# Cached-key expansion beside prefill attention: a third squares buffer, an earlier split of the next stream, and scores issued behind the value products

## The reference

```python
def mla_expand(c_kv, w_kv_b, k_norm):
    b, S, _ = c_kv.shape
    kvb = (c_kv @ w_kv_b).reshape(b, S, MLA_HEADS, QK_NOPE + V_HEAD)   # 16 heads, 64 + 64
    k_nope = rmsnorm(kvb[..., :QK_NOPE], k_norm)
    return k_nope, kvb[..., QK_NOPE:]

def attend(q_nope, q_rope, k_nope, k_rope, v, q_pos, k_pos):
    s = (einsum(q_nope, k_nope) + einsum(q_rope, k_rope)) * ATTN_SCALE
    mask = (k_pos // CHUNK)[None, :] <= (q_pos // CHUNK)[:, None]
    p = softmax(where(mask, s, -inf), axis=-1)
    return einsum(p, v)
```

## Time and profile before

| | us |
|---|---|
| median of 3 runs (1838.54 to 1841.67) | 1838.8 |
| the profiled execution | 1838.99 |
| its span | 1837.2 |
| TensorE busy in the span | 1809.3 |
| VectorE busy | 1135.8 |
| ScalarE busy | 827.9 |
| GpSimd busy | 228.9 |

### The profile page before, as it was taken

The page is one execution under the profiler, slowest core; times in us unless marked ns, Lnnn a source line. Parts: engine busy times, 40 slices in busy tenths (PEclk is TensorE's granted clock), DMA queues, the critical chain, the costliest instruction groups (busy, mean ns, idle before and its releaser), DMA issues.

```text
span 1837.2 us, 28276 instructions
## 1 busy us (share of the span) xinstructions
PE 1809.3 (98%) x10567; PEld 1732.5 (94%) x10567; DVE 1135.8 (62%) x1706; ACT 827.9 (45%) x1420; POOL 228.9 (12%) x280
## 2 busy tenths in 40 slices
PE   9999999999999999999999999999998999999998
PEld 9999999799888999999999999996777999999998
DVE  6454447879889645444775454456778856454445
ACT  6333336665564433333553333346665544333333
POOL 1000110311311000011400001122112131000110
PEclk9999999999999999999999999999999999999999
DMA  6434444456352544454344434451124534444442
GB/s 212 135 117 136 139 138 153 153 207 235 122 206 87 193 125 127 124 149 138 115 143 118 135 116 140 139 170 40 47 85 142 166 116 127 133 120 131 143 137 76
DMA packets 68452, 249.48 MB, mean 136 GB/s; under 512 B 8264, under 2 KB 10568, under 8 KB 67088
## 3 DMA queue, kind: packets, MB, share of 16 engines
q1 hardware_dynamic: 58880, 206.86, 36.8%
q0 software_dynamic: 9488, 41.48, 6.6%
HBM read 235.51 MB, written 12.12 MB: 135 GB/s over the span
## 4 chain that ended last, share of the span: by engine, by line
PE 82%; DVE 10%; ACT 3%; DMA 2%; issue 2%; POOL 0%; SPq 0%; DVEq 0%; ACTq 0%; POOLq 0%
PE pair L1913 24%; PE pair L1914 24%; PE pair L1915 24%; DVE wlo L1245 2%; PE pair L2333 2%; PE pair L2335 2%; PE pair L2334 2%; DVE cy L1372 1%; DMA lowA<-in_cacheT 1%; DVE S L1468 1%; PE pair L2422 1%; PE pair L1920 0%; PE pair L1922 0%; PE pair L1921 0%; PE pair L2121 0%
## 5 line engine op out<-in xcount | busy, mean ns | idle before, releaser
L1913 PE MATMUL pair<-xh,whi 128*128 128x384 f32 x1960 | 660.3, 337 | 3.0 <-DVE xl L1255 2.0
L1915 PE MATMUL pair<-xh,wlo 128*128 128x384 f32 x1960 | 654.9, 334 | 0.0
L1914 PE MATMUL pair<-xl,whi 128*128 128x384 f32 x1960 | 654.8, 334 | 0.0
L1245 DVE TENSOR_TENSOR wlo<-raw,whi 128x1024 fp32r<-128x1024 f32 (+3 forms) x371 | 463.8, 1252 | 160.7 <-ACT whi L708 159.8
L708 ACT ACTIVATE whi<-raw 128x1024 fp32r<-128x1024 f32 (+2 forms) x369 | 378.0, 1028 | 261.9 <-PE pair L1915 257.8
L1913 PEld LDWEIGHTS pair<-xh,whi 128*128 128x128 f32 x1960 | 367.9, 188 | 10.0 <-DVE wlo L1245 3.9
L1914 PEld LDWEIGHTS pair<-xl,whi 128*128 128x128 f32 x1960 | 368.0, 188 | 1.6 <-issue 1.0
L1915 PEld LDWEIGHTS pair<-xh,wlo 128*128 128x128 f32 x1960 | 367.9, 188 | 0.0
L1265 DVE TENSOR_TENSOR tg<-pair,rstd 128x384 f32<-128x384 f32 x88 | 49.1, 558 | 326.2 <-PE pair L1915 325.5
L1913 PE MATMUL pair<-ah,whi 128*128 128x384 f32 x704 | 235.2, 334 | 0.0
L1914 PE MATMUL pair<-al,whi 128*128 128x384 f32 x704 | 235.1, 334 | 0.0
(11 more groups left out here) (408 smaller groups left out, 2202.2 us busy)
## 6 DMA issues: line engine op xcount, KB each, us to landing
raw<-in_stream SPq DMA_DIRECT2D x372, 512.0 KB, 3.6
S<-in_ssm POOLq DMA_DIRECT2D x4, 2048.0 KB, 9.3
out_ssm_s<-S POOLq DMA_DIRECT2D x4, 2048.0 KB, 7.8
seg<-acs_rows POOLq DMA_DIRECT2D x12, 512.0 KB, 6.0
cTb<-in_cacheT POOLq DMA_DIRECT2D x10, 512.0 KB, 4.3
kn<-rs_rows SPq DMA_DIRECT2D x16, 264.0 KB
lowC<-in_cache SPq DMA_DIRECT2D x8, 512.0 KB, 3.2
lowA<-in_cacheT POOLq DMA_DIRECT2D x6, 512.0 KB, 5.0
```

The source lines that it names most:

```text
L1245: V.tensor_tensor(wlo[:, r, 0:w], raw[:, r, 0:w], whi[:, r, 0:w].bitcast(F32), ALU.subtract).then_inc(lo_ready, 1)
L1913: M(out, whi[:, r, ws], mh_(k), start=first and k == k0, stop=False)
L1914: M(out, whi[:, r, ws], ml_(k), start=False, stop=False)
L1915: ins = M(out, wlo[:, r, ws], mh_(k), start=False, stop=last and k == k1 - 1)
```

## The change

Three edits. The squares get three slots of 512 columns in `kn` in place of two, so a square waits for the row sum of three products back. `past_split(y + 1)` moves ahead: on ScalarE from behind the output copy to the place before the square of product 8y + 3, on VectorE from behind the output's low part to the place behind the row sum of product 8y + 4. And TensorE issues the scores of two heads right behind the value products of a turn, where they stood at the head of the next turn; only heads 2 and 3 stay at the head of turn 0. Scores of turn y are thus those of heads 2y + 4 and 2y + 5.

```diff
--- before.py
+++ after.py
@@ -1077,11 +1077,11 @@
 
             def past_square(w):
                 act.wait_ge(past_ps, w + 1)
-                if w < 2:
+                if w < 3:
                     act.wait_ge(key_turn_ps, 4)
                 else:
-                    act.wait_ge(past_sum, w - 1)
-                A(kn[:, w % 2, 0:512], bank[w % 2][:, :], ACT.Square).then_inc(past_sq, 1)
+                    act.wait_ge(past_sum, w - 2)
+                A(knf[:, 512 * (w % 3):512 * (w % 3) + 512], bank[w % 2][:, :], ACT.Square).then_inc(past_sq, 1)
 
             def p_exp(x):
                 s, o = x % 2, 48 + 8 * (x % 2)
@@ -1121,6 +1121,8 @@
                 p_turned(2 * y + 1)
                 if y == 0:
                     A(rsT2[0:MH, P:2 * P], bank[2][0:MH, 384:512], ACT.Copy).then_inc(rs_ev, 1)
+                if 2 <= y + 1 < STREAMS:
+                    past_split(y + 1)
                 past_square(8 * y + 3)
                 if y + 1 < MH // 2:
                     p_exp(2 * y + 2)
@@ -1135,8 +1137,6 @@
                 past_square(8 * y + 5)
                 act.wait_ge(po_ps, 2 * y + 2)
                 A(xh[:, y, 0:SEQ], bank[7 if y % 2 else 3][:, 0:SEQ], ACT.Copy).then_inc(oh_ready, 1)
-                if 2 <= y + 1 < STREAMS:
-                    past_split(y + 1)
                 past_square(8 * y + 6)
                 if y in (1, 2):
                     z = (xh, xl)[y - 1]
@@ -1755,7 +1755,7 @@
             def past_sums(w):
                 b, st, g = w // 8, w // 2 % 4, w % 2
                 dve.wait_ge(past_sq, w + 1)
-                V.reduce_sum(ksq[:, st, b, 8 * g:8 * g + 8], kn[:, w % 2, 0:512].rearrange("p (h d) -> p h d", h=8),
+                V.reduce_sum(ksq[:, st, b, 8 * g:8 * g + 8], knf[:, 512 * (w % 3):512 * (w % 3) + 512].rearrange("p (h d) -> p h d", h=8),
                              axis=AX.X).then_inc(past_sum, 1)
 
             def p_max(x):
@@ -1805,14 +1805,14 @@
                         p_max(2 * y + 2)
                     if i == 3 and more:
                         p_max(2 * y + 3)
+                    if i == 4 and 2 <= y + 1 < STREAMS:
+                        past_split(y + 1)
                     if i == 5:
                         if more:
                             p_norm(2 * y + 2)
                         dve.wait_ge(oh_ready, y + 1)
                         V.tensor_tensor(xl[:, y, 0:SEQ], bank[7 if y % 2 else 3][:, 0:SEQ], xh[:, y, 0:SEQ].bitcast(F32),
                                         ALU.subtract).then_inc(ol_ready, 1)
-                        if 2 <= y + 1 < STREAMS:
-                            past_split(y + 1)
                     if i == 6 and more:
                         p_norm(2 * y + 3)
                     if y in (3, 4) and i == 0:
@@ -2344,9 +2344,9 @@
             p_values(3)
             pe.wait_ge(wk_lo, 2)
             for y in range(MH // 2):
-                for x in (2 * y + 2, 2 * y + 3):
-                    if x < MH:
-                        p_scores(x)
+                if y == 0:
+                    p_scores(2)
+                    p_scores(3)
                 for i in range(4):
                     past_expand(8 * y + i)
                 if y == 0:
@@ -2371,6 +2371,9 @@
                                 start=k == 0, stop=at != 1)
                         if at == 2:
                             ins.then_inc(po_ps, 1)
+                for x in (2 * y + 4, 2 * y + 5):
+                    if x < MH:
+                        p_scores(x)
                 if y == MH // 2 - 1:
                     pe.wait_ge(past_rstd, 3)
                     rs_turn(bank[2], 0, 6)
```

## The result

The changed kernel takes 1843.38 us (median of 12 runs, 1842.07 to 1844.25) against 1838.45 us of the kernel before in the same comparison. The ratio is 1.0028 with a 95% interval of 1.002 to 1.0035: slower by 4.9 us, with 1844.5 forecast and 1840 to 1848 as the range.

The account below looks back on a forecast made before the run. TensorE, busy 98% of the span, was taken as the bound, so each new wait is lost. Terms 4.75 + 1.71 - 0.74 gave +5.7 us, hence 1844.5 us from a median of 1838.8; range 1840 to 1848.

Parts of the forecast that it names:

- The split ahead of the square: ScalarE's split delays the square that product 8y + 5 waits for: 0.95 us in turns 1, 2, 4, 5, 6; 4.75 in sum.
- e5: Product 8y + 5 on TensorE, six matmuls; forecast to wait for the delayed square, second matmul 0.95 us late in turn 1.
- the price by the row: 0.95 us per stall of TensorE behind the split, counting the weight load itself as waiting, as the trace row shows.
- the lower one of 0.84: Price per stall if TensorE hid the weight load in the wait; whole forecast about 0.8 us less.
- Pass 3 with its late load: Turn 3: the split's 0.95 us plus 0.76 waiting for stream 4's load, 1.71 lost; between 1.0 and 2.9 by landings.
- The low part earlier: VectorE's split moved ahead ends TensorE's waits at the ends of turns 3 and 6: together -0.74 us.
- The value for pass 7: Third product of turn 7 waits for a square behind the square-root table load, giving back 0.80 of turn 6's 1.23 us.
- The third slot at 0, the scores at 0: Third buffer of squares: 0, bound 0 to -0.3 us. Scores behind value products: 0, bounds -1.6 to +0.6 us.
- Sum: All terms for the kernel: 4.75 + 1.71 - 0.74 = +5.7 us, predicting 1844.5 us.
- The rivals: Split hidden, 1837.3 to 1838.1 (0.11); scores fill value-product idle, 1842.9 (0.13); more late loads, 1845.7 up to 1848 (0.10).
- the shift of 0.83 us for the load of stream 4: With the scores moved, stream 4's load lands 0.83 us later relative to turn 3, so the split waits 0.76 us.
- e6: Product 8y + 6 on TensorE, six matmuls, behind the value products; with the scores ahead of it, 1.33 us nearer the next turn.

Follow-up runs that it names:

- the first two experiments: Changed kernel with ScalarE's split behind the square of product 8y + 3: 1836.72 us; with half the split ahead of that square, half behind: 1840.4 us.
- the four runs on them: Kernel before with only the split moved 1842.59 us, only the scores moved 1838.88, only the third slot 1838.87; changed kernel with two slots 1843.34.
- the split alone: Kernel before with only past_split moved, on ScalarE and VectorE; two slots, scores at the head of the turn: 1842.59 us, ratio 1.0031.
- the load first: Changed kernel with GpSimd's load of stream 4 issued ahead of the four small copies: 1843.62 us, ratio 1.0029.

## Why the prediction was right, term by term

- *The split ahead of the square, 0.95 us in each pass.* Right, and the mechanism is shown by the first two experiments. Measured 0.94 in passes 1, 4, 5 and 6 and 1.08 in pass 2: 4.84 for the five passes, 4.75 forecast. After the wait the first matmul of e5 starts together with its load, 0.84 us behind its beat (1295.81 by 1294.65 and five beats), and the second follows 0.33 us later in place of 0.23 (1296.65 to 1296.98). So the price by the row was right and the lower one of 0.84, with the load hidden, was not.
- *Pass 3 with its late load.* The mechanism was right, the size was not: 1.37 in place of 1.71. The issue stood 2.87 us behind the second matmul of the pass (2.88 forecast), but the load landed in 4.2 us where I had taken the 4.5 of the kernel before. These 0.3 us are nearly the whole miss. The wait itself was 0.32 and not 0.76, since the split could start only 0.90 us behind the copies even without it (see the open point below); that 0.14 is lost either way. The range given, 1.0 to 2.9, held it.
- *The low part earlier.* The term came out as -1.06, forecast -0.74. The 0.31 of pass 3 and the 1.23 of pass 6 were won, but pass 7 gave back 0.48 and not 0.80. The value for pass 7 is what was mis-sized: I read the square at 1375.60 as waiting for the table load, while it waited for its own product, whose last matmul ended then (1375.17 + 0.39). In the changed kernel the square follows the root by 0.43 us (1379.90 to 1380.33), and that is the queue's own pace.
- *The third slot at 0, the scores at 0.* Right in the changed kernel, by the four runs on them. In the kernel before, the scores' move alone costs 0.8 us of the stage by way of the copies; in the changed kernel the earlier low part hides all of it but the load's wait.
- *Sum.* 4.84 + 1.37 - 1.06 = 5.15 in the stage against +5.7; in the time +4.9 against +5.7. The first term came out 0.09 higher than forecast and the next two both lower, so the sum is not right by errors that cancel.

The rivals are out: pass 1 took 15.02 us and not 14.1 or 14.7, and no split but that of pass 3 waited for its load.

What the prediction left out is the second transfer in GpSimd's queue. It had seen the shift of 0.83 us for the load of stream 4, but not that VectorE waits for the copies ahead of it, 1.26 us in the kernel before and 2.14 in the changed one.

One thing stays open. In passes 1, 4, 5 and 6 the split starts 0.75 or 0.76 us after the start of ScalarE's first copy, but 0.90 in pass 2 of the changed kernel:

```profile
1309.35 0.87 ACT L1101 ACTIVATE rstd<-pair 128x384 f32<-128x384 f32 x2 [1.13 <-PE pair L2359]
...
1310.25 1.06 ACT L1076 ACTIVATE cTh<-cTb 128x1024 fp32r<-128x1024 f32 x1
```

It is 0.90 in pass 3 as well, where no load is waited for (the split alone, the load first). With no split between, in the kernel before, the square follows by 0.75 or 0.76 in passes 2 and 3 too. It adds about 0.14 to each of the two passes in every kernel that has the split there. No run here tells why.

## What to carry to other kernels

Before something is moved ahead in an engine's queue, look at the instruction that it is moved in front of, and measure from its end to the start of whoever waits for it: here it was 0.05 us, and a copy of 0.95 us moved in front of it cost 0.94 us in most passes, while one line further down it cost nothing, as value products and scores covered it. A move that takes work away from between two transfers and their use (the scores, here) also shortens the time that those transfers have. And where an engine has two reasons to wait, read which of them ends last before a price is put on the other.

## What the runs showed of the hardware

- An fp32r matmul of 512 columns keeps a beat of 0.232 us in this stage (six in 1.39). After a wait the matmul starts together with its weight load, and the second matmul comes 0.33 or 0.34 us behind. So a first matmul that is 0.84 us late made the second 0.94 late (pass 1 of the changed kernel).
- Value products of 64 output columns cost 1.01 us in the kernel before. Together with the scores they cost the same within 0.03 us in all kernels, whether the scores stood right behind them (3.70 to 3.73 from e5 to e6, but for the one wait for a mask) or a pass's head away (2.40 and 1.33). The idle time of the weight loads before them in pass 1 was 0.36 us with an expansion product behind (the kernel before) and 0.37 with scores behind (the changed kernel).
- A 512 KB load of cached latents took 3.8 to 5.6 us from issue to landing in the passes of all kernels; those of more than 4.7 are all of stream 2, in pass 1. Four copies of 128 KB each landed 2.3 to 2.5 us after their issue when they stood ahead of such a load, and 4.3 to 4.4 when they stood right behind it; their reader then waited 4.58 us in place of 2.14.
